# A decoder layer in split float32: weight slots and the second activation buffer at other byte offsets in SBUF

## What is computed

```python
h = rms_norm(x, attn_norm)
q_r, k_r, v_r, g_r, q_m, k_m, v_m = split(h @ w_in)          # 1024 x 6144
y_ret  = (group_norm(retention(rotary(q_r), rotary(k_r), v_r)) * silu(g_r)) @ w_ret_o
y_moba = softmax_attention(rms_norm(q_m), rms_norm(k_m), v_m) @ w_moba_o
gate_ret, gate_moba = split(sigmoid(h @ w_gate + b_gate))    # 1024 x 2048
x = x + (gate_ret * y_ret + gate_moba * y_moba) @ w_out
h = rms_norm(x, ffn_norm)
u_gate, u_val = split(causal_conv3(h @ w_up))                # 1024 x 5632
x = x + (silu(u_gate) * u_val) @ w_down                      # 2816 x 1024
```

## Time and profile before

| | |
|---|---|
| time, median of 3 runs | 488.76 us |
| the three runs | 488.94, 486.81, 488.76 us |
| span of the profiled execution (the only time that the profile has of it) | 486.9 us |
| TensorE: matmuls busy, share of the span, count | 475.4 us, 98%, 3183 |
| TensorE: weight loads busy | 439.7 us, 90% |
| VectorE busy | 296.1 us, 61% |
| ScalarE busy | 249.0 us, 51% |
| GpSimd busy | 17.1 us, 4% |
| DMA moved | 86.65 MB, mean 178 GB/s |
| mean granted TensorE clock | 0.993 of full speed |

### The profile page before, as it was taken

How to read it: one execution, slowest core, us unless ns; L and a number is a source line. 1 busy time by engine, 2 the same in 40 slices (tenths; PEclk the granted TensorE clock), 3 DMA queues, 4 the chain that set the end, 5 groups by cost and what they waited for, 6 DMA issues and landing times.

```text
span 486.9 us, 7961 instructions
## 1 busy us (share of the span) xinstructions
PE 475.4 (98%) x3183; PEld 439.7 (90%) x3183; DVE 296.1 (61%) x354; ACT 249.0 (51%) x354; POOL 17.1 (4%) x26
## 2 busy tenths in 40 slices
PE   6999999999999999999999989999999999999997
PEld 4789999888888999999999868999999999988885
DVE  3854884574665546355337856488888777886312
ACT  3735332345884739333444625566666666673310
POOL 1000000311110001000000010000000000000000
PEclk9999999999999999999999997999999999999999
DMA  8996255144455524843453562144545555539002
GB/s 314 355 346 256 104 199 224 48 139 166 168 172 187 219 114 142 333 168 133 165 195 131 194 228 105 69 172 172 176 181 187 194 194 192 189 132 363 3 1 86
DMA packets 13400, 86.65 MB, mean 178 GB/s; under 512 B 1472, under 2 KB 1856, under 8 KB 3648
## 3 DMA queue, kind: packets, MB, share of 16 engines
q1 hardware_dynamic: 12096, 82.84, 45.7%
q10 hardware_dynamic: 864, 1.88, 1.1%
q0 software_dynamic: 416, 1.57, 0.9%
HBM read 85.24 MB, written 1.05 MB: 177 GB/s over the span
## 4 chain that ended last, share of the span: by engine, by line
PE 95%; DMA 1%; DVE 1%; ACT 1%; issue 0%; POOL 0%; POOLq 0%; SPq 0%
PE bank L333 18%; PE bank L334 18%; PE bank L335 18%; PE bank L293 7%; PE bank L295 7%; PE bank L294 7%; PE bank L526 4%; PE bank L523 4%; PE bank L524 4%; PE bank L350 2%; DMA xs<-x_dram 1%; PE bank L429 1%; PE bank L411 1%; PE bank L430 0%; PE bank L410 0%
## 5 line engine op out<-in xcount | busy, mean ns | idle before, releaser
L775 DVE TENSOR_TENSOR w_lo<-w_raw,w_hi 128x2048 fp32r<-128x2048 f32 x75 | 170.3, 2288 | 79.5 <-ACT w_hi L548 79.4
L333 PE MATMUL bank<-h_hi,w_hi 128*128 128x256 f32 x608 | 173.5, 285 | 0.7 <-DVE h_lo L980 0.7
L334 PE MATMUL bank<-h_lo,w_hi 128*128 128x256 f32 x608 | 172.7, 284 | 0.0
L335 PE MATMUL bank<-h_hi,w_lo 128*128 128x256 f32 x608 | 172.7, 284 | 0.0
L548 ACT ACTIVATE w_hi<-w_raw 128x2048 fp32r<-128x2048 f32 x75 | 141.6, 1915 | 33.4 <-PE bank L526 16.9
L333 PEld LDWEIGHTS bank<-h_hi,w_hi 128*128 128x128 f32 x608 | 117.5, 193 | 1.2 <-issue 1.1
L334 PEld LDWEIGHTS bank<-h_lo,w_hi 128*128 128x128 f32 x608 | 117.5, 193 | 0.1
L335 PEld LDWEIGHTS bank<-h_hi,w_lo 128*128 128x128 f32 x608 | 117.4, 193 | 0.0
L293 PE MATMUL bank<-w_hi,h_hi 128*128 128x512 f32 x160 | 63.1, 395 | 0.3 <-DVE w_lo L780 0.2
L295 PE MATMUL bank<-w_hi,h_lo 128*128 128x512 f32 x160 | 62.4, 390 | 0.0
L294 PE MATMUL bank<-w_lo,h_hi 128*128 128x512 f32 x160 | 62.3, 389 | 0.0
(11 more groups left out here) (112 smaller groups left out, 435.4 us busy)
## 6 DMA issues: line engine op xcount, KB each, us to landing
w_raw<-weights_dram SPq DMA_DIRECT2D x76, 1024.0 KB, 4.9
xs<-x_dram SPq DMA_DIRECT2D x2, 512.0 KB, 5.2
w_raw<-weights_dram SPq DMA_DIRECT2D x2, 512.0 KB, 8.3
xs<-x_dram POOLq DMA_DIRECT2D x1, 1024.0 KB, 7.9
out_dram<-ys SPq DMA_DIRECT2D x4, 256.0 KB, 2.0
area<-decay_dram ACTq DMA_DIRECT2D x1, 768.0 KB, 4.1
area<-gain_rows_dram ACTq DMA_DIRECT2D x1, 512.0 KB, 7.0
area<-gain_rows_dram POOLq DMA_DIRECT2D x1, 512.0 KB, 10.7
```

What stands on the lines that cost most here:

```text
L333: mm(o, s_hi, r_hi[:, k, :], start=(k == 0 and m % 2 == 0), stop=False)
L334: mm(o, s_hi, r_lo[:, k, :], start=False, stop=False)
L335: ins = mm(o, s_lo, r_hi[:, k, :], start=False, stop=(k == KT - 1 and m % 2 == 1))
L775: tt(w_lo[r][:, :], raw[r][:, :], w_hi[r][:, :].bitcast(f32), ALU.subtract).then_inc(lo_ready, 1)
```

## The change

Sizes and starts of four SBUF tensors; no instruction is added, removed or moved. The list of instructions of each of the five engines (with their operands' shapes and the order) is the same before and after, row by row; only the addresses in them differ.

```diff
+STAGGER = 4
...
-        w_hi = [sb(f"w_hi{r}", [P, HALF_ELEMS], f32r) for r in range(SLOTS)]
-        w_lo = [sb(f"w_lo{r}", [P, HALF_ELEMS], f32r) for r in range(SLOTS)]
+        w_hi_all, w_lo_all = (sb(name, [P, SLOTS * (HALF_ELEMS + STAGGER)], f32r) for name in ("w_hi", "w_lo"))
+
+        def staggered(whole, r):
+
+            first = (HALF_ELEMS + STAGGER) * r
+            return whole[:, first:first + HALF_ELEMS]
+
+        w_hi = [staggered(w_hi_all, r) for r in range(SLOTS)]
+        w_lo = [staggered(w_lo_all, r) for r in range(SLOTS)]
...
-        a_hi = sb("a_hi", [P, D_FF // P, SEQ], f32r)
-        a_lo = sb("a_lo", [P, D_FF // P, SEQ], f32r)
+        a_whole = [sb(name, [P, D_FF // P * SEQ + 2 * STAGGER], f32r) for name in ("a_hi", "a_lo")]
+        a_hi, a_lo = (w[:, STAGGER:STAGGER + D_FF // P * SEQ].rearrange("p (k s) -> p k s", s=SEQ) for w in a_whole)
```

## The result

| | before | after |
|---|---|---|
| median | 488.05 us (19 runs, 486.65 to 488.99) | 488.90 us (19 runs, 488.26 to 490.25) |
| ratio | | 1.002, 95% interval 1.0011 to 1.003 |
| span of the profiled execution | 486.9 us | 487.3 us |

The changed kernel is slower by 0.2%, about 0.9 us: less than the 0.5% that the prediction called the limit of one measurement, but clear of zero with 19 runs on either side. The forecast was 488.7 us and no change.

What follows compares the result with a forecast made beforehand. TensorE's unbroken matmul stream was taken as the bound; terms of 0 + 0 + 0 left the profiled execution at 486.9 us, and the median lying 1.9 us over it gave 488.7 us, range 485.8 to 493.8 (forecast's own 486.2 to 491.2).

Steps and rivals of the forecast that it cites:

- What bounds the kernel: Whole kernel: TensorE's matmul stream bounds it, busy 475.4 of 486.9 us, with 8.2 us of waits at norms and start.
- The splits and the loads: VectorE's and ScalarE's splits on shifted slots: at most 1.1 us, covered by TensorE's stream; loads cost 0.
- rival C: Up projection: VectorE's splits stretch and become the bound; doubled, 12.5 us more, 501.2 us; chance 0.04.
- what a shifted matmul costs ... I take 0: TensorE matmuls with a shifted operand: 0 change of pace, since VectorE's and ScalarE's rows at varied starts show 0.
- The bounds: Shifted matmuls: at most 18.9 us lost to one more 64-byte fetch, or 31.3 us gained if the fixed part vanished.
- four things: All that can change: pace of shifted matmuls, VectorE's and ScalarE's instructions on moved tensors, their mutual effects, loads; sum 0.
- Counting the touched matmuls modulo 64: All matmuls: 2352 of 2952 counted as having at least one operand at a shifted start.
- Rival A: Shifted matmuls and their weight loads: one fetch more, 1.67 ns a piece, 4.7 us, 493.4 us; chance 0.17.
- Rival B: TensorE matmuls: the fixed part is a collision of equal starts; up to 31.3 us freed, 457.4 us; chance 0.08.
- the 13.3 ns: Fixed part of every TensorE matmul at full clock: 120.0 ns for 256 columns less 106.7 for the columns.

Runs made afterwards that it cites:

- stagger_kept: Kernel before with only the 16-byte stagger of the weight slots; w_lo, h and a at their former places modulo 256, a not shifted; ratio 1.0031 (1.0011 to 1.0052).
- near64: Kernel before with 64 bytes of padding ahead of w_hi and 192 ahead of h_hi; ratio 0.9788, and 0.9793 when repeated word for word.

## Why the prediction was wrong, step by step

- **What bounds the kernel**: right. TensorE had no spare time, no wait appeared or grew, and the difference of the spans (+0.4 us) is that of TensorE's steps. A detail was misread: of the 8.2 us of waits 0.5 (for `a_lo`, L919, at 206 us) lie in the attention and not at a norm or the start.
- **The splits and the loads**: right. 2288 ns for VectorE's split before and after; rival C did not occur. VectorE's L1019 and ScalarE's L726 were good rows for VectorE and ScalarE.
- **The step that failed is "what a shifted matmul costs ... I take 0"**, taken from those same rows of two other engines. In its place: -1.6 ns on average for the 2208 matmuls of 256 columns, +5.2 ns for the 744 of 512, two terms of 3.5 and 3.9 us that all but cancel (+0.4 us, of which 0.3 is half clock). That the sum is near 0 is luck: it is the difference of two larger numbers, neither of them zero. The bounds (18.9 us up, 31.3 down) held both.
- **The list of what can change was short of one thing, the clock.** The prediction names four things and has no term for how long TensorE runs at half clock, though the earlier trace rows show such a stretch. The measured +0.9 us of the medians lies in the stated range, but it comes mostly from there: at the same granted clock the difference is 0.3 us or less, and 0 of 19 executions kept the full clock, against 24 of 78 of the kernel before. That the stagger causes this is likely from those counts; the mechanism stays open.
- **Counting the touched matmuls modulo 64** failed too: 600 of the 2952 were taken to be untouched, among them slot 0 of the up projection (117.2 ns instead of 120.0). All were touched, since `w_lo` and `h` moved by 64 and 128 bytes and `a_hi` and `a_lo` by 144 and 176.
- **Rival A** asked for slot 0 at 120.0 and the others above it; stagger_kept shows 120.0 in slot 0 and less in the others for 256 columns. What holds of A is its sign for 512 columns, at 4 to 8 ns instead of its 1.67.
- **Rival B** named the right quantity, the relation between the two starts, and the wrong law. Among starts at multiples of 64, distance 0 costs the most ns with 256 columns and the fewest with 512, and of the 13.3 ns at most 6.7 go (120.0 - 113.3 ns), not all. For this change it gave 3.5 us back and not 31; near64, with 256 bytes of padding, gets 12 us out of the same quantity in the faster of its profiles.
- **The rules of the Trainium skill.** The Trainium skill gives SBUF lines of 16 bytes ("SBUF — State Buffer", Specifications (TRN2)), and the prediction took from that that a stagger of 16 bytes changes nothing; stagger_kept shows 118.4 against 120.0 and 231.5 to 233.4 against 228.2 ns, so the measurement decides against using that rule here. The Trainium skill's fixed part of about 2.5 ns ("TensorE: Matmul & The Clock Gate", "Wait — 56ns, not 53.3ns?") is for bf16; in fp32r no layout measured here came under 6.7 ns with 256 columns or 13.3 with 512.

## What to carry to other kernels

In a stream of fp32r matmuls that never waits, look at the distance between two starts for each width, and compare it with columns times the price of one: what is left over is where layout can pay. Here the distance between the stationary and the moving buffer, modulo 256 bytes, was worth up to 6.7 ns of 120 with 256 columns, and cost 2 to 7 ns of 227 with 512, so widths must be weighed against each other before a layout is chosen. An engine's indifference to an alignment says nothing of another engine, and a total that doesn't move can hide two terms that do. Before a difference of a few tenths of a percent is put down to an edit, compare executions with the same granted clock, and take more than one profile where a stream can have two paces.

## What the runs showed of the hardware that was not expected

- The pace of an fp32r matmul stream at full clock depends on stationary minus moving start with a period of 256 bytes (0: 120.0 and 226.7 ns; 64: 113.4 and 233.2; 192: 117.8 and 229.1 for 256 and 512 columns), and on what ran ahead of the stream (64: 113.4 or 117.8; 128: 118.3 or 120.2).
- At a distance of 64 there are two states (of TensorE's own stream, each with its pace), 113.3 and 117.8 ns (at 192 with 512 columns 228.9 and 233.3), kept for a hundred microseconds and more; one odd matmul can switch them, and executions of the same program lay up to 8.6 us apart (475.7 to 484.3), some of it by the granted clock.
- A moving start 8 bytes off a multiple of 64 gave 126.6 ns, the slowest of all pairs with 256 columns; such a start on VectorE or ScalarE cost nothing (476 to 487 ns at all starts, 600 against 597).
- How long an execution runs at half clock differs between executions of one program (mean granted clock 0.989 to 1.000, 486.2 to 490.3 us for the kernel before), and the staggered layouts kept the full clock in 1 of 43 executions, the kernel before in 24 of 78.
